# The recurrence's gate products written as three fp32r products of divided operands

## The chip, the cores and the metric

The kernel runs on one core of one Trainium2 chip. Its time is the device time of one execution in microseconds (us). A core has a matrix engine (PE, TensorE), a vector engine (DVE), an activation engine (ACT), a general engine (POOL, GpSimd) and a queue engine (SP) that here issues every DMA. The engines run side by side, each in its own program order, and wait for each other through semaphores.

## What is computed

One layer of a hybrid model on 1280 tokens: 1024 latent tokens and 256 context tokens, of width 1024. A projection feeds three branches: a long convolution (Hyena), a Fourier mixing (FNet) and a bidirectional gated recurrence (RG-LRU). Then follow a merge, an output projection and a feed-forward part. The change is in the recurrence. Cut to what matters:

```python
def rglru_scan(x, w_r, b_r, w_i, b_i, lam, h0, reverse, reset):
    xb = x.reshape(B, L, N_RG_BLOCKS, RG_BLOCK)          # 8 blocks of 128 channels
    r = sigmoid(einsum('blnc,ncd->blnd', xb, w_r) + b_r)
    i = sigmoid(einsum('blnc,ncd->blnd', xb, w_i) + b_i)
    log_a = -RG_C * r * softplus(-lam)
    a = exp(log_a)
    mult = sqrt(-expm1(2.0 * log_a))
    h = scan(h[t] = a[t] * h[t-1] + mult[t] * (i[t] * x[t]))   # forward and backward

xr = depthwise_conv(u_rx, rcw, rcb, ...)                  # 4 taps along the tokens
h_f = rglru_scan(xr, wr[0], ..., False, reset)
h_b = rglru_scan(xr, wr[1], ..., True, reset)
y_c = ((h_f + h_b) * gelu(u_ry)) @ w_c
```

The einsums are the gate products: in each of the 8 blocks, xr (128 channels by 1280 tokens) meets four 128x128 matrices, one for r and one for i in each direction.

## The kernel before

The activations lie with channels on the 128 partitions and tokens along the row. The 1280 tokens are cut in three pieces of 512, 512 and 256 columns. All big projections run as "split products": a weight tile and the input are each divided into a rounded part (fp32r, "hi") and the remainder ("lo"), and three fp32r matmuls, hi*hi, hi*lo and lo*hi, are added up in PSUM (`split_product`, lines 860 to 862). The input pairs h_hi and h_lo are made once. The weight tiles come from memory one by one: SP loads tile t into one of two buffers w_raw, POOL makes w_hi and w_lo from it in two instructions (lines 789 and 792), PE uses them. A tile of 128x1024 makes eight split products on each piece.

The stage of the change is the second one, `Fori(0, KD // 2) as m` with two halves s on every engine: eight passes n = 2m + s, one for each channel block of the recurrence, each with two projection tiles. What each engine does in pass n, in its order:

- PE: tile 2n+16 (it gives the recurrence's input `rin`), in an odd pass the FNet token matmuls, tile 2n+17 (it gives `g_ry`), a wait for xr, the 12 gate products (line 1042, plain fp32 in one call each), and in an even pass the FNet channel matmuls (line 1013).
- ACT: `rin` from PSUM (line 1247), FNet token copies in an odd pass, a wait for the pass before to have ended (`zc_ready`), gelu into `g_ry` (1316), 12 sigmoids that take the gate products (1324), then exp, tanh, square and root (1330 to 1336), and FNet copies in an even pass.
- DVE: the depthwise convolution that makes xr (1588, 1593), in an even pass the FNet first stage (lines 244 to 256, its result `fn_a` is PE's input at line 1013), then the recurrence (1712 to 1731). At its end it raises `zc_ready`. Only then does it start on the xr of the next pass.
- SP: it waits for `zc_ready` of the pass, stores the result, and only then issues the loads of the following pass: in its order FNet's input, the next `rpack` and the two weight tiles. `rpack` holds the four gate matrices and the vectors of a block; that of pass n is loaded during pass n-1.
- POOL: one loop that rounds and divides tile after tile. For tile t it waits until PE has finished tile t-2 (`proj_done[2]`), whose buffers it reuses, and until the new raw tile has landed.

So in pass n POOL divides tiles 2n+18 and 2n+19, the two of the next pass, whose loads SP issues after pass n-1 has ended.

In the trace a pass begins when DVE has ended the one before: the ends of passes 0, 1, 2 and 3 stand at 633.1, 680.7, 723.7 and 772.8 us. From pass 2 on, an even and an odd pass together take the same time again, 92.1 us.

Of the kernel before, what the change touches and what calls it, by code (L numbers as in the profile page):

```python
# [8 lines left out]
F32 = mybir.dt.float32  # L28
# [31 lines left out]

# [7 lines left out]

# [11 lines left out]

# [8 lines left out]


def real_dft_even(o, z, temp, out):


    e, d = temp(0, 4), temp(4, 8)
    o.add(e, z(0, 4), z(4, 8))
    o.sub(d, z(0, 4), z(4, 8))
    o.sub(out("re4"), temp(0), temp(2))
    o.sub(out("im4"), temp(3), temp(1))
    o.add(temp(8, 10), temp(0, 2), temp(2, 4))
    o.sub(temp(10), temp(5), temp(7))  # L100
    o.add(temp(11), temp(5), temp(7))
    o.add(out("re0"), temp(8), temp(9))
    o.sub(out("re8"), temp(8), temp(9))
    o.mul_add(out("re2"), temp(10), COS[2], temp(4))
    o.mul_add(out("re6"), temp(10), -COS[2], temp(4))
    o.mul_add(out("im6"), temp(11), -COS[2], temp(6))
    o.mul_sub(out("im2"), temp(11), -COS[2], temp(6))

# [28 lines left out]

# [6 lines left out]

# [46 lines left out]

# [7 lines left out]

class Chain:  # L200


# [9 lines left out]
    def loose(self, ins):  # L212


        ins.then_inc(self.sem, 1)
        self.n += 1
        if self.n > 1:
            self.eng.wait_ge(self.sem, self.n - 1)
# [16 lines left out]

class Butterfly:


# [19 lines left out]

class MixUnits:


# [17 lines left out]

# [10 lines left out]

def spectrum_places(buf):


    def at(name):
        if name.startswith("c"):
            return buf[:, 9 + int(name[3:]), :] if name[1:3] == "re" else buf[:, 19, :]
        f = int(name[2:])
        return buf[:, f if name[:2] == "re" else 11 + f, :]
    return at

# [14 lines left out]


# [4 lines left out]


def build_program(nc, dr):

    ctx = ExitStack()
    with ctx:
        def sem(name):
            return ctx.enter_context(nc.semaphore(name))

        def sb(stack, name, shape, dt=F32):  # L330
            return stack.enter_context(nc.sbuf_tensor(name, shape, dt))

# [20 lines left out]

# [49 lines left out]
        rpack = [sb(st, f"rpack{s}", [P, R_ALL]) for s in range(2)]  # L403
        for buf, name in ((r_b, "r_b"), (i_b, "i_b"), (a_b, "a_b")):
            buf.append(sb(st, f"{name}1", [P, T]))
# [14 lines left out]

# [15 lines left out]

# [9 lines left out]


# [21 lines left out]

# [45 lines left out]
        xr_ready = sem("xr_ready")  # L515
# [23 lines left out]


# [19 lines left out]
        def raw_z(n):  # L560


            if n == 2:
                return v_b, v_in, 16 * (CH + 1), 0
            if n < 2:
                return zraw[n], zraw_in[n], 16, 0
            slot = (n - 3) % 2
            return zraw[slot], zraw_in[slot], 16 * ((n - 3) // 2 + 2), n - 2 if n < 5 else n - 1
# [3 lines left out]

# [75 lines left out]

# [31 lines left out]

# [6 lines left out]

# [45 lines left out]

# [39 lines left out]


        @block.gpsimd
        def _(pool):
# [51 lines left out]
            with pool.Fori(TILES_L1 // 2 + 1, OUT_TILE0 // 2 + 1) as m:  # L828
                for s in range(2):

                    pool.wait_ge(proj_done[2], 2 * m + s)
                    split(2 * m + s, s, w_hi[s], w_lo[s])
# [6 lines left out]
            for q in range(FFN_TILES):  # L839


                if q < 2:
                    pool.wait_ge(proj_done[2], OUT_TILE0 + 1 + 31 + q)
                split(MIX_TILES + q, q, wf_hi[q], wf_lo[q])
# [7 lines left out]


        @block.tensor
        def _(pe):
# [8 lines left out]
            def projection(use, ws, xs, cols, made=None, pieces=(0, 1, 2)):  # L864


                for b in pieces:
                    a, e, _ = PIECES[b]

                    pe.wait_ge(proj_free[b], use)  # L870
                    for k, (w, x) in enumerate(zip(ws, xs)):
                        if made:
                            pe.wait_ge(made, len(xs) * b + k + 1)
                        ins = split_product(ps[b][:, 0:e - a], [w[0][:, cols[k]], w[1][:, cols[k]]],
                                            [x[0][:, a:e], x[1][:, a:e]], k == 0, k == len(ws) - 1)
                    ins.then_inc(proj_done[b], 1)
# [34 lines left out]

# [29 lines left out]

# [53 lines left out]

# [34 lines left out]
            with pe.Fori(0, KD // 2) as m:  # L1030
                for s in range(2):
                    n = 2 * m + s
                    projection_tile(2 * n + L2_TILE0, 0)
                    if s == 1:
                        fnet_tokens(m)
                    projection_tile(2 * n + (L2_TILE0 + 1), 1)
                    pe.wait_ge(xr_ready, n + 2)
                    pe.wait_ge(rpack_in[s], 16 * m + 16)
                    for j in range(12):
                        out, done = mix_unit(u2, m, RG_UNIT[s] + j)  # L1040
                        a, e, _ = PIECES[j % 3]
                        mm(out[:, 0:e - a], rpack[s][:, (j // 3) * P:(j // 3 + 1) * P], xr[:, a:e],
                           start=True, stop=True).then_inc(done, 1)
                    if s == 0:
                        fnet_channels(m)

# [42 lines left out]

# [36 lines left out]

# [41 lines left out]

        @block.scalar
        def _(act):  # L1170
# [15 lines left out]

# [53 lines left out]

# [39 lines left out]

# [24 lines left out]
            with act.Fori(0, KD // 2) as m:  # L1305
                for s in range(2):
# [4 lines left out]
                    if s == 1:  # L1311
                        take_fnet_tokens(m)
                    act.wait_ge(zc_ready, n + 1)
# [26 lines left out]

# [38 lines left out]

# [30 lines left out]

# [34 lines left out]

# [16 lines left out]


        @block.vector
        def _(dve):
# [16 lines left out]

# [28 lines left out]


# [170 lines left out]

# [15 lines left out]
            with dve.Fori(0, KD // 2) as m:  # L1699
                for s in range(2):  # L1700
# [5 lines left out]
                              pack[:, R_CONVB:R_CONVB + 1], 4, 2, xr_ready)  # L1706
                    if s == 0:
                        fnet_first_stage(m)
# [25 lines left out]

# [36 lines left out]

# [79 lines left out]

# [65 lines left out]


def dft_constants():

# [23 lines left out]

# [14 lines left out]

# [3 lines left out]

# [5 lines left out]

# [75 lines left out]
```

## Time and profile before

| | before |
|---|---|
| device time, median of 3 runs (lowest, highest) | 2820.89 us (2819.37, 2822.51) |
| span of the profiled execution, first to last instruction | 2818.3 us |
| PE busy | 2576.4 us, 91% |
| PE loading weights | 2141.8 us, 76% |
| DVE busy | 1579.7 us, 56% |
| POOL busy | 884.1 us, 31% |
| ACT busy | 559.6 us, 20% |
| mean granted PE clock | 0.961 |

The span is 2.6 us shorter than the median of the timed runs: what lies around the span. Busy shares are averages over stages with different limits. The stage of the change runs from about 572 to 957 us. PE's matmuls are pipelined, so that two in a row overlap in the records; the distance between two starts is what one costs. An fp32 matmul leaves two records for each call. A clock of 1.00 is 2.4 GHz and one of 0.50 is 1.2 GHz.

### The profile page before, as it was taken

The page shows a single profiled execution, that of the slowest core. Times are in us where ns is not written, and L with a number is a line of the kernel's source. Part 1 is how long each engine was busy: PE and PEld are TensorE (multiplying, and loading weights), DVE is VectorE, ACT ScalarE, POOL GpSimd, SP SyncE. Part 2 cuts the span into 40 slices and gives each one's busy share as a digit, 9 for nine tenths or more (in the row PEclk, how much of TensorE's full clock was granted, in tenths as well). Part 3 has the DMA queues.
Part 4 walks back from the last instruction along what each step waited for, and adds up shares of the span by engine and source line. Part 5 has one row for each costly group of instructions (what it writes and reads, how often), then busy time and mean ns, then how long its engine had stood idle before and what let it go on. Part 6 is the DMA issues. An engine that isn't in the chain of part 4 may idle for free. (4 is left out here: it accounts for less than half of the span.)

```text
span 2818.3 us, 34644 instructions
## 1 busy us (share of the span) xinstructions
PE 2576.4 (91%) x13422; PEld 2141.8 (76%) x13422; DVE 1579.7 (56%) x2636; ACT 559.6 (20%) x825; POOL 884.1 (31%) x483
## 2 busy tenths in 40 slices
PE   6599998999999799999987998979999999999995
PEld 2377776786877688878876887858888888888885
DVE  6888888856568466665666445383322233332227
ACT  3201101045565421122221001130000000000002
POOL 0355455622121122322232332333323133323220
PEclk9799999999999899999998999989999999999998
DMA  6222333122112322222235323211011011101002
GB/s 263 79 96 105 127 122 126 56 96 75 44 68 70 144 92 99 100 91 91 91 119 207 129 86 103 84 45 45 30 45 35 24 45 45 45 30 45 22 22 75
DMA packets 53536, 233.49 MB, mean 83 GB/s; under 512 B 6628, under 2 KB 8548, under 8 KB 47861
## 3 DMA queue, kind: packets, MB, share of 16 engines
q1 hardware_dynamic: 53492, 232.93, 23.0%
q8 instruction: 26, 0.43, 0.1%
q14 instruction: 18, 0.14, 0.0%
HBM read 178.37 MB, written 54.53 MB: 83 GB/s over the span
## 5 line engine op out<-in xcount | busy, mean ns | idle before, releaser
L860 PE MATMUL ps<-h_hi,w_hi 128*128 128x512 f32 (+1 forms) x2256 | 812.1, 360 | 42.5 <-DVE h_lo L1570 18.4
L861 PE MATMUL ps<-h_lo,w_hi 128*128 128x512 f32 (+1 forms) x2256 | 802.4, 356 | 0.0
L862 PE MATMUL ps<-h_hi,w_lo 128*128 128x512 f32 (+1 forms) x2256 | 801.6, 355 | 0.0
L789 POOL TENSOR_TENSOR w_hi<-w_raw,zero_col 128x1024 fp32r<-128x1024 f32 x102 | 229.2, 2247 | 1576.3 <-PE ps L862 1118.0
L860 PEld LDWEIGHTS ps<-h_hi,w_hi 128*128 128x128 f32 x2256 | 428.4, 190 | 116.8 <-issue 28.9
L862 PEld LDWEIGHTS ps<-h_hi,w_lo 128*128 128x128 f32 x2256 | 428.3, 190 | 60.6
L861 PEld LDWEIGHTS ps<-h_lo,w_hi 128*128 128x128 f32 x2256 | 428.9, 190 | 58.4
L1862 DVE TENSOR_TENSOR a<-sil,ps 128x512 f32<-128x512 f32 (+1 forms) x66 | 39.5, 598 | 506.2 <-PE ps L862 505.0
L792 POOL TENSOR_TENSOR w_lo<-w_raw,w_hi 128x1024 fp32r<-128x1024 f32 x102 | 277.1, 2716 | 8.0
L1896 DVE SCALAR_TENSOR_TENSOR x<-ps,mod,x 128x512 f32<-128x512 f32 (+1 forms) x264 | 172.1, 661 | 95.0 <-PE ps L862 94.4
L861 PE MATMUL ps<-h_lo,wf_hi 128*128 128x512 f32 (+1 forms) x528 | 188.7, 357 | 0.0
L860 PE MATMUL ps<-h_hi,wf_hi 128*128 128x512 f32 (+1 forms) x528 | 188.7, 357 | 0.0
L862 PE MATMUL ps<-h_hi,wf_lo 128*128 128x512 f32 (+1 forms) x528 | 188.7, 357 | 0.0
L862 PE MATMUL ps<-act_hi,wf_lo 128*128 128x512 f32 (+1 forms) x528 | 187.0, 354 | 0.0
L861 PE MATMUL ps<-act_lo,wf_hi 128*128 128x512 f32 (+1 forms) x528 | 187.0, 354 | 0.0
L860 PE MATMUL ps<-act_hi,wf_hi 128*128 128x512 f32 (+1 forms) x528 | 186.8, 354 | 0.0
L1429 ACT ACTIVATE sil<-ps 128x512 f32<-128x512 f32 (+1 forms) x66 | 34.7, 527 | 763.1 <-PE ps L862 763.1
L789 POOL TENSOR_TENSOR wf_hi<-w_raw,zero_col 128x1024 fp32r<-128x1024 f32 x44 | 86.2, 1960 | 180.0 <-PE ps L862 180.0
L953 PE MATMUL ps<-f_a,fwd 128*128 128x128 f32 x640 | 90.1, 310 | 53.9 <-DVEq L1650 53.3
L953 PEld LDWEIGHTS ps<-f_a,fwd 128*128 128x128 f32 x640 | 87.9, 225 | 57.3 <-issue 50.3
L860 PEld LDWEIGHTS ps<-h_hi,wf_hi 128*128 128x128 f32 x528 | 100.0, 189 | 15.7
L862 PEld LDWEIGHTS ps<-h_hi,wf_lo 128*128 128x128 f32 x528 | 99.3, 188 | 15.9
(238 smaller groups left out, 3807.7 us busy)
## 6 DMA issues: line engine op xcount, KB each, us to landing
w_raw<-in_weights SPq DMA_DIRECT2D x146, 512.0 KB, 3.7
ada_w<-in_w_ada SPq DMA_DIRECT2D x20, 1024.0 KB, 6.2
scratch_gate_s<-g_st SPq DMA_DIRECT2D x24, 640.0 KB, 3.3
side<-scratch_gate_s SPq DMA_DIRECT2D x24, 640.0 KB, 3.9
scratch_k_s<-kstage SPq DMA_DIRECT2D x8, 1536.0 KB, 5.1
hy_k<-scratch_k_s SPq DMA_DIRECT2D x8, 1536.0 KB, 8.8
scratch_hy_s<-hout SPq DMA_DIRECT2D x16, 640.0 KB, 3.2
x_in<-in_x SPq DMA_DIRECT2D x8, 640.0 KB, 9.1
```

Of the source, the lines that this page charges most:

```text
L789: nc.gpsimd.tensor_tensor(hi[:], w_raw[slot % 2][:], zero_col[:].to_broadcast([P, D]), ALU.add).then_inc(pool_step, 1)
L792: nc.gpsimd.tensor_tensor(lo[:], w_raw[slot % 2][:], hi[:].bitcast(F32), ALU.subtract).then_inc(split_done, 1)
L860: mm(out, w_pair[0], x_pair[0], start=first, stop=False)
L861: mm(out, w_pair[0], x_pair[1], start=False, stop=False)
L862: return mm(out, w_pair[1], x_pair[0], start=False, stop=last)
L953: ins = mm(o, mats[:, q, m, :], part, start=n == 0, stop=n == len(terms) - 1)
L1429: fn(sil[n % 2][:, 0:e - a], ps[b][:, 0:e - a], ACT.Silu).then_inc(f_free[b], 1)
L1862: tt(a32[n % 2][:, 0:e - a], sil[n % 2][:, 0:e - a], ps[ub][:, 0:e - a], ALU.mult).then_inc(f_free[ub], 1)
L1896: stt(x1[:, m, a:e], ps[b][:, 0:e - a], mod[:, 5 * KD + m, seq:seq + 1], x1[:, m, a:e], ALU.mult, ALU.add).then_inc(f_free[b], 1)
```

## The change

It does these things:

- the gate matrices of a pass are divided by POOL into `rm_hi` and `rm_lo` (128x512 each), in two new instructions between the division of tile 2n+18 and that of tile 2n+19; there is one pair of buffers for all passes
- xr is divided into `xr_hi` by ACT (one copy of 128x1280, after it has waited for xr, ahead of the gelu) and into `xr_lo` by DVE (one subtraction of 128x1280, after it has waited for `xr_hi`, ahead of FNet's first stage)
- PE waits for both divisions, and each of the 12 fp32 gate products becomes three fp32r matmuls
- the DMA scratch (`dynamic_dma_scratch_size`) is set to 2048, which makes room for the new buffers

```diff
+        xr_hi, xr_lo = sb(st, "xr_hi", [P, T], F32R), sb(st, "xr_lo", [P, T], F32R)
+        rm_hi, rm_lo = sb(st, "rm_hi", [P, 4 * P], F32R), sb(st, "rm_lo", [P, 4 * P], F32R)
...
         def _(pool):
-            with pool.Fori(TILES_L1 // 2 + 1, OUT_TILE0 // 2 + 1) as m:
+            def split_gates(n, s, loads):
+                pool.wait_ge(rpack_in[s], loads)
+                nc.gpsimd.tensor_tensor(rm_hi[:], rpack[s][:, 0:4 * P], zero_col[:].to_broadcast([P, 4 * P]),
+                                        ALU.add).then_inc(rm_rounded, 1)
+                pool.wait_ge(rm_rounded, n + 1)
+                nc.gpsimd.tensor_tensor(rm_lo[:], rpack[s][:, 0:4 * P], rm_hi[:].bitcast(F32),
+                                        ALU.subtract).then_inc(rm_split, 1)
+            with pool.Fori(0, KD // 2) as m:
+                for s in range(2):
+                    n = 2 * m + s
+                    for q in range(2):
+                        pool.wait_ge(proj_done[2], 2 * n + (TILES_L1 + 2 + q))
+                        split(2 * n + (TILES_L1 + 2 + q), q, w_hi[q], w_lo[q])
+                        if q == 0:
+                            split_gates(n, s, 16 * m + 16)
+            with pool.Fori((TILES_L1 + TILES_L2) // 2 + 1, OUT_TILE0 // 2 + 1) as m:
...
         def _(pe):
-                    pe.wait_ge(xr_ready, n + 2)
-                    pe.wait_ge(rpack_in[s], 16 * m + 16)
+                    pe.wait_ge(xr_split, n + 1)
+                    pe.wait_ge(rm_split, n + 1)
                     for j in range(12):
                         out, done = mix_unit(u2, m, RG_UNIT[s] + j)
                         a, e, _ = PIECES[j % 3]
-                        mm(out[:, 0:e - a], rpack[s][:, (j // 3) * P:(j // 3 + 1) * P], xr[:, a:e],
-                           start=True, stop=True).then_inc(done, 1)
+                        cols = slice((j // 3) * P, (j // 3 + 1) * P)
+                        split_product(out[:, 0:e - a], [rm_hi[:, cols], rm_lo[:, cols]],
+                                      [xr_hi[:, a:e], xr_lo[:, a:e]], True, True).then_inc(done, 1)
...
         def _(act):
+                    act.wait_ge(xr_ready, n + 2)
+                    fn(xr_hi[:], xr[:], ACT.Copy).then_inc(xr_rounded, 1)
                     act.wait_ge(zc_ready, n + 1)
...
         def _(dve):
+                    dve.wait_ge(xr_rounded, n + 1)
+                    tt(xr_lo[:], xr[:], xr_hi[:].bitcast(F32), ALU.subtract).then_inc(xr_split, 1)
...
-    nc = bacc.Bacc("TRN2", target_bir_lowering=False, num_devices=1)
+    nc = bacc.Bacc("TRN2", target_bir_lowering=False, num_devices=1, dynamic_dma_scratch_size=2048)
```

On POOL, in one odd pass of the second stage, the order of before is this (w_raw is the landed weight tile; raw_in0 and raw_in1 are the landings of its two buffers, proj_done2 is PE's end of a tile):

```order
L788 ISA [waits proj_done2]
L789 TENSOR_TENSOR w_hi<-w_raw,zero_col 128x1024 [waits raw_in0]
L791 REGISTER_ALU
L792 TENSOR_TENSOR w_lo<-w_raw,w_hi 128x1024 [waits pool_step]
L788 ISA [waits proj_done2]
L789 TENSOR_TENSOR w_hi<-w_raw,zero_col 128x1024 [waits raw_in1]
L791 REGISTER_ALU
L792 TENSOR_TENSOR w_lo<-w_raw,w_hi 128x1024 [waits pool_step]
```

The same place of the changed kernel:

```order
L729 ISA [waits proj_done2]
L730 TENSOR_TENSOR w_hi<-w_raw,zero_col 128x1024 [waits raw_in0]
L732 REGISTER_ALU
L733 TENSOR_TENSOR w_lo<-w_raw,w_hi 128x1024 [waits pool_step]
L773 TENSOR_TENSOR rm_hi<-rpack,zero_col 128x512 [waits rpack_in1]
L775 REGISTER_ALU
L776 TENSOR_TENSOR rm_lo<-rpack,rm_hi 128x512 [waits rm_rounded]
L729 ISA [waits proj_done2]
L730 TENSOR_TENSOR w_hi<-w_raw,zero_col 128x1024 [waits raw_in1]
L732 REGISTER_ALU
L733 TENSOR_TENSOR w_lo<-w_raw,w_hi 128x1024 [waits pool_step]
```

The division of this pass's gate matrices stands behind the division of the next pass's first tile, and with it behind that tile's landing.

On PE, at the end of a pass's second tile, the order of before:

```order
L862 MATMUL ps<-h_hi,w_lo 128x256
L1037 REGISTER_ALU
L1038 ISA [waits xr_ready]
L888 ISA [waits rpack_in0]
L1042 MATMUL ps<-xr,rpack 128x512 [waits mix_free0]
L1042 MATMUL ps<-xr,rpack 128x512 [waits mix_free1]
```

And of the changed kernel:

```order
L820 MATMUL ps<-h_hi,w_lo 128x256
L991 REGISTER_ALU
L845 ISA [waits rm_split,xr_split]
L818 MATMUL ps<-xr_hi,rm_hi 128x512 [waits mix_free0]
L819 MATMUL ps<-xr_lo,rm_hi 128x512
L820 MATMUL ps<-xr_hi,rm_lo 128x512
```

The wait for xr and for the landed rpack has become a wait for what DVE and POOL make of them.

On DVE, behind the convolution in an even pass, the order of before:

```order
L1593 SCALAR_TENSOR_TENSOR xr<-rin,rpack,xr 128x1024 [waits dve_step]
L1593 SCALAR_TENSOR_TENSOR xr<-rin,rpack,xr 128x256
L244 TENSOR_TENSOR fn_c<-fn_u 128x512 [waits dve_step,fn_in]
L247 TENSOR_TENSOR fn_c<-fn_u 128x512 [waits dve_step]
```

And of the changed kernel:

```order
L1535 SCALAR_TENSOR_TENSOR xr<-rin,rpack,xr 128x1024 [waits dve_step]
L1535 SCALAR_TENSOR_TENSOR xr<-rin,rpack,xr 128x256
L1648 REGISTER_ALU [waits dve_step]
L1649 TENSOR_TENSOR xr_lo<-xr,xr_hi 128x1280 [waits xr_rounded]
L208 TENSOR_TENSOR fn_c<-fn_u 128x512 [waits fn_in]
L211 TENSOR_TENSOR fn_c<-fn_u 128x512 [waits dve_step]
```

FNet's first stage now stands behind ACT's rounding of xr and behind the subtraction.

## Rows read from the trace of the kernel before

**Rows 1.** The page: its head, then its first part, the engines' busy times.
```profile
span 2818.3 us, 34644 instructions
...
PE 2576.4 (91%) x13422; PEld 2141.8 (76%) x13422; DVE 1579.7 (56%) x2636; ACT 559.6 (20%) x825; POOL 884.1 (31%) x483
```

**Rows 2.** Who waited for whom, on PE: us in total, times, longest.
```profile
PE ps L1064 <- DMA v_b<-scratch_hy_s: 16.8, 1, 16.8
...
PE ps L1042 <- DVEq L1596: 13.1, 3, 4.4
```

**Rows 3.** Timeline of DVE, passes 1 to 3: start, length, what, [idle before].
```profile
679.19 1.49 DVE L1731 TENSOR_TENSOR r_b<-r_b,g_ry 128x1280 f32<-128x1280 f32 x1 [0.22 <-DVE r_b L1729]
...
682.82 5.12 DVE L1593 SCALAR_TENSOR_TENSOR xr<-rin,rpack,xr 128x1024 f32<-128x1024 f32 x6
...
691.41 2.57 DVE L244 TENSOR_TENSOR fn_c<-fn_c 128x256 f32<-128x256 f32 x1
...
699.57 0.28 DVE L247 TENSOR_TENSOR fn_a<-fn_u 128x128 f32<-128x128 f32 x1
...
722.23 1.49 DVE L1731 TENSOR_TENSOR r_b<-r_b,g_ry 128x1280 f32<-128x1280 f32 x1 [0.22 <-DVE r_b L1729]
...
725.42 5.11 DVE L1593 SCALAR_TENSOR_TENSOR xr<-rin,rpack,xr 128x1024 f32<-128x1024 f32 x6
```

**Rows 4.** Timeline of PE around the gate products of pass 3, an odd one.
```profile
735.97 0.39 PE L862 MATMUL ps<-h_hi,w_lo 128*128 128x512 f32 x1
736.20 0.28 PE L860 MATMUL ps<-h_hi,w_hi 128*128 128x256 f32 x1
736.31 0.28 PE L861 MATMUL ps<-h_lo,w_hi 128*128 128x256 f32 x1
...
739.07 8.75 PE L1042 MATMUL ps<-xr,rpack 128*128 128x512 f32 x24
747.47 0.58 PE L860 MATMUL ps<-h_hi,w_hi 128*128 128x512 f32 x1
```

**Rows 5.** Timeline of all engines in pass 2, an even one: ACT and PE.
```profile
698.38 1.05 ACT L1324 ACTIVATE i_b<-ps,rpack 128x512 f32<-128x512 f32 x2 [0.17 <-PE ps L1042]
...
700.02 7.17 PE L1013 MATMUL ps<-fn_ch,fn_a 128*128 128x256 f32 x32 [1.25 <-DVEq L1697]
...
703.39 1.27 ACT L1333 ACTIVATE r_b<-a_b 128x1280 f32<-128x1280 f32 x1
```

**Rows 6.** Timeline of POOL: passes 0, 2 and 3.
```profile
597.90 2.53 POOL L789 TENSOR_TENSOR w_hi<-w_raw,zero_col 128x1024 fp32r<-128x1024 f32 x1 [26.57 <-DMA w_raw<-in_weights]
...
604.79 3.48 POOL L792 TENSOR_TENSOR w_lo<-w_raw,w_hi 128x1024 fp32r<-128x1024 f32 x1
...
689.06 2.07 POOL L789 TENSOR_TENSOR w_hi<-w_raw,zero_col 128x1024 fp32r<-128x1024 f32 x1 [37.44 <-DMA w_raw<-in_weights]
691.22 2.48 POOL L792 TENSOR_TENSOR w_lo<-w_raw,w_hi 128x1024 fp32r<-128x1024 f32 x1
...
730.44 1.89 POOL L789 TENSOR_TENSOR w_hi<-w_raw,zero_col 128x1024 fp32r<-128x1024 f32 x1 [32.15 <-DMA w_raw<-in_weights]
```

**Rows 7.** Timeline of SP, pass 2: the issue of the next pass's two weight tiles.
```profile
683.13 0.86 SPq L578 DMA_DIRECT2D w_raw<-in_weights  x2
```

**Rows 8.** Timeline of DVE, pass 0.
```profile
604.57 1.49 DVE L1712 TENSOR_TENSOR i_b<-i_b,xr 128x1280 f32<-128x1280 f32 x1 [5.90 <-ACT i_b L1324]
```

**Rows 9.** Groups by line, POOL, shapes apart: count, busy us, mean ns.
```profile
L813 POOL TENSOR_TENSOR hout<-hout,hy_part 128x256 f32<-128x256 f32 x80 | 68.4, 855 | 6.7
```

**Rows 10.** Timeline of PE, pass 0.
```profile
599.42 8.76 PE L1042 MATMUL ps<-xr,rpack 128*128 128x512 f32 x24
608.02 7.07 PE L1013 MATMUL ps<-fn_ch,fn_a 128*128 128x256 f32 x32
```

**Rows 11.** Sums by stretch: length, busy of PE, PEld, DVE, ACT, POOL, granted clock.
```profile
688.00:692.00 4.00, 3.78 (x7) 1.88 (x8) 3.91 (x5) 1.34 (x2) 2.86 (x2) 0.62 0.35 143
...
255.00:259.00 4.00, 4.00 (x19) 4.00 (x20) 3.63 (x3) 0.00 (x0) 3.63 (x5) 0.52 0.17 72
```

More of the change, by code:

```diff
@@ L513, in build_program @@
         k_ready = sem("k_ready")
-        xr_ready = sem("xr_ready")
+        xr_ready, xr_rounded, xr_split = sem("xr_ready"), sem("xr_rounded"), sem("xr_split")
+        rm_rounded, rm_split = sem("rm_rounded"), sem("rm_split")
         a2_ready = sem("a2_ready")
```

## The prediction

> **What bounds the kernel now.** I read the page first: PE is busy 91% of the span, DVE 56%, POOL 31% [rows 1]. That makes PE the engine to save on, and gate products that cost less would be a gain. But the share is an average, so I went to the waits of PE next, to see whether PE sets the end in the stage that is changed. It doesn't quite: three times PE stands 4.4 us in front of the gate products, 13.1 us in all, until DVE has made xr, and at the end of the stage it stands 16.8 us for a load that SP issues only after the last pass of DVE [rows 2]. So the end of the stage is the end of DVE's pass 7, and every wait of PE before it counts only by what it does to that.
>
> The timelines show the loop behind it. Pass 1 ends on DVE at 680.7, the convolution that makes xr runs until 687.9, pass 2 ends at 723.7, and the convolution of pass 3 runs until 730.5 [rows 3]. In an even pass PE waits for xr, its gate products end at 698.8, ACT's last sigmoid at 699.4, and the FNet channel matmuls start at 700.0, when DVE has ended FNet's first stage [rows 3, 5]. Two tiles later PE reaches the gate products of pass 3 at 739.1, 8.5 us after xr is there: odd passes are bound by PE. The end of an odd pass follows its sigmoids at a fixed distance and starts the next even one. That loop, all engines in turn, is the bound.
>
> **The matmuls themselves: a gain.** A block of 12 gate products takes 8.4 us at full clock, from 739.07 to 747.47 [rows 4]. In fp32r, matmuls start 0.23 us apart at 512 columns and 0.12 apart at 256 [rows 4]. A block then has 24 of the first and 12 of the second: 24 x 0.227 + 12 x 0.12 = 6.9 us. That is 1.5 us less, and in an odd pass the first fp32r matmul behind the block, 0.58 us long in place of 0.39, gives some 0.2 back too. ACT follows the products and could take off a little less; I take 1.6 us for an odd pass and 1.5 for an even one. Were nothing else changed, the eight blocks would give 12 to 13 us.
>
> **The division of xr: two steps ahead of PE and of FNet.** ACT's copy of 128x1280 costs 1.3 us, as the square of the same size [rows 5], DVE's subtraction 1.5 us, as the product of the same size [rows 8]; with two hand-overs xr is divided 3.0 us after it is made. In odd passes the 8.5 us of slack hide it. In even passes it would put the gate products at 690.9 instead of 688.2. ACT's gelu and sigmoid table load, which now stand behind the copy, are done by 693.5. Behind DVE's wait is FNet's first stage, and it starts 3 us later.
>
> **The division of the gate matrices: where the wait is.** POOL executes in order. It divides the next pass's first tile, then this pass's gate matrices. That tile's load is issued by SP after the end of the pass before, at 683.1 in pass 2 [rows 7], and POOL, idle for 37.4 us, starts on it at 689.06 [rows 6]. The gate matrices were loaded a pass ago, but they are queued behind it. Counting on POOL: w_hi 1.9 to 2.1, w_lo 2.35 to 2.5 [rows 6], then two instructions of 512 columns. No row has these; half of the large ones is 1.0 and 1.2 us, and an instruction of 256 columns takes 0.86 [rows 9], so together they lie between 1.7 and 4.5. I take 2.3, half of the large ones, since the small one lies only little below. Undisturbed, the gate matrices are ready 6.8 us after the landing: 695.8.
>
> It won't be undisturbed. While POOL works, DVE's small operations of some 0.4 us are stretched to 2.57 us [rows 3], about the length of one POOL instruction; and a POOL w_lo that started 0.2 us into DVE's 1.49 us product took 3.48 instead of 2.4 [rows 6, 8]. So the two alternate by whole instructions. xr_lo now falls into POOL's w_hi, runs when that has ended, and holds up w_lo by 1.5 us; one or two FNet operations get in between, 0.7 us. That gives 698.0 for the start of the gate products in pass 2, 9.8 us later than before.
>
> The Trainium skill, "SBUF — State Buffer", section "Who interferes with whom", says that a DVE instruction with two SBUF inputs and a GpSimd instruction that reads SBUF exclude each other for a whole instruction. By that rule xr_lo costs POOL its full 1.5 us and 698.0 stands; without it the undisturbed 695.8 would be the number. The trace agrees, with the 3.48 us.
>
> From there: the block takes 6.9 us plus what the clock takes. After the 4.4 us wait of before, the granted clock was 0.62 in the 4 us behind it, and after a 6.2 us wait of an earlier stage it was 0.52 in the 4 us behind it [rows 11]; either way some 3.4 to 4 us of work at 1.2 GHz, or 1.7 to 2 us lost. In pass 2 that loss was there before. So the block ends at 698.0 + 6.9 + 1.7 = 706.6, 7.8 us later than 698.8. DVE has ended FNet's first stage by about 705, since POOL is at work until 703. The FNet matmuls start at 706.8 instead of 700.0: PE goes on 6.8 us later, and the pass, behind its sigmoids, ends 7.8 us later.
>
> **The odd pass behind it.** PE arrives at 745.9 instead of 739.1. POOL, from a landing at 730.4 + 7.8, needs 6.7 us and up to 1.5 more for xr_lo: 744.9 to 746.4. That is a draw; I add 0.3. The block saves 1.6. So an even and an odd pass together take 6.8 + 0.3 - 1.6 = 5.5 us more. There are three such pairs (passes 2 to 7): 16.5 us.
>
> **The first pair.** In pass 0 nothing waited. The tile lands at 597.90 [rows 6], the gate products started at 599.42 [rows 10]. Now they start 7.4 us after the landing, at 605.3, 5.9 us later, with a wait long enough to lose the clock: 6.9 + 2.0 us for the block, which ends at 614.2 instead of 608.0 [rows 10], 6.2 us later. In pass 1 the draw again, 0.7 here, minus 1.6: 5.3 us.
>
> **The rest.** The DMA scratch: every transfer of this kernel is issued by SP, none by POOL, and no row prices the scratch; I take nothing. The same page, section "SBUF size: 192, 224, or 256?", says that this scratch belongs to descriptors made on GpSimd, which no run here shows. The tiles 2n+19, divided after the gate matrices, are ready at 703 and needed at about 732. The later stages start from the load at the end of pass 7 [rows 2] and are only shifted.
>
> **Sum.** 5.3 + 16.5 = 21.8 us. The span of 2818.3 us [rows 1] becomes 2840.1; with the 2.6 us around it, which the median has too, 2842.7, so 2843.
>
> Bounds: with an undisturbed POOL (695.8) and no draw lost, a pair costs 4.5 - 1.6 = 2.9 and the first 3.8: 12.5 us, 2833. With more DVE operations in between (699.5) and 1.5 us lost in each odd pass, a pair costs 8.2 and the first 7.5: 32 us, 2853.
>
> **The rivals.** First, POOL is not late, and only the division of xr stands in the way. Then an even block starts at 690.9 and ends 0.8 us later than before; FNet's stage, 3 us later under POOL's work, puts PE 2.6 us back, less 1.6 in the odd pass: 1.0 us a pair, and the first pair gains 3.2. Together about 0: 2821. For it: odd passes have slack and the matrices lie there early. Against it: the order of POOL and the landing at 689.06 after an idle time of 37 us. 7 in 100.
>
> Second, faster: both divisions are hidden and the blocks give their 12 to 13 us, 2808. It needs the gate matrices and xr divided before PE arrives at 683.8 in an even pass, when xr is only made at 687.9. 6 in 100.
>
> Third, slower still: the clock. With 14 us of waiting in an even pass PE might run the whole block at 1.2 GHz, 6.9 us lost in place of 1.7, in four passes: 20 us more, 2863. It decides from the point where the clock stays low for over 4 us of work after a wait; the 6.2 us wait of an earlier stage shows 4 [rows 11]. 7 in 100.
>
> **How the numbers follow.** The forecast with its bounds has 80 in 100, the rivals 20. The range of 2833 to 2853 is the forecast's own; I widen it by 2 us below for a landing that comes sooner: 2831 to 2853. Beyond about 0.2%, 5.6 us, a measurement of this kernel can tell a change. Slower takes in the forecast and the third rival, 0.87; within 0.2%: 0.07; faster: 0.06.
>
> **What would show it.** In the profile after, the longest waits of PE before the gate products should end on POOL's rm_lo, four of them in even passes, some 14 us each in passes 2, 4 and 6 and 6 us in pass 0; small ones in odd passes. POOL's order should show w_hi, w_lo, rm_hi, rm_lo directly behind the landing. A pair should take 97.6 us instead of 92.1. A block should take 6.9 us in odd passes. If PE waits for xr_lo instead, the first rival holds; if it doesn't wait at all, the second.

## The result

The changed kernel takes 2842.28 us, the median of 4 runs (2839.52 to 2848.59), beside 2821.33 us for the kernel before. The ratio is 1.0077, with a 95% interval of 1.0063 to 1.0091: it is slower by 21 us, or 0.8%. The forecast was 2843 us. The four runs lie 9 us apart, and the profiled one is the fastest of them (2839.5 us).

The page of the changed kernel, its head and the busy times, beside [rows 1]:

```profile
span 2837.7 us, 34885 instructions
...
PE 2566.2 (90%) x13518; PEld 2155.8 (76%) x13518; DVE 1611.1 (57%) x2644; ACT 569.3 (20%) x833; POOL 911.0 (32%) x499
```

PE is busy for 10 us less than before, in a span that is 19 us longer. The gain on the matmuls is there and doesn't decide the time. The waits of PE, beside [rows 2] (us in total, times, longest):

```profile
PE ps L818 <- POOL rm_lo L776: 46.1, 4, 14.6
...
PE ps L1018 <- DMA v_b<-scratch_hy_s: 16.7, 1, 16.7
```

The three waits for xr, 13.1 us, are gone. Four waits for POOL's rm_lo, 46.1 us, stand in their place. The wait for v_b at the end of the stage is as long as before, so the stage in front of it has grown as a whole: the first matmul on v_b starts at 984.6 us in place of 962.6, 22.0 us later.

POOL in passes 2 and 3, beside [rows 6] (start, length, what, idle before):

```profile
691.11 1.89 POOL L730 TENSOR_TENSOR w_hi<-w_raw,zero_col 128x1024 fp32r<-128x1024 f32 x1 [36.13 <-DMA w_raw<-in_weights]
693.08 3.47 POOL L733 TENSOR_TENSOR w_lo<-w_raw,w_hi 128x1024 fp32r<-128x1024 f32 x1
696.51 1.49 POOL L773 TENSOR_TENSOR rm_hi<-rpack,zero_col 128x512 fp32r<-128x512 f32 x1
698.08 1.59 POOL L776 TENSOR_TENSOR rm_lo<-rpack,rm_hi 128x512 fp32r<-128x512 f32 x1
699.63 1.94 POOL L730 TENSOR_TENSOR w_hi<-w_raw,zero_col 128x1024 fp32r<-128x1024 f32 x1
...
747.54 1.28 POOL L776 TENSOR_TENSOR rm_lo<-rpack,rm_hi 128x512 fp32r<-128x512 f32 x1
```

The gate matrices had been loaded in the pass before, and POOL stood idle for 36 us. It was waiting for the landing of a tile of the next pass, which nobody needed yet. And PE, where those instructions end:

```profile
699.90 0.79 PE L818 MATMUL ps<-xr_hi,rm_hi 128*128 128x512 f32 x1 [13.76 <-POOL rm_lo L776]
...
709.32 2.97 PE L967 MATMUL ps<-fn_ch,fn_a 128*128 128x256 f32 x13
```

The gate products start when rm_lo has ended. On DVE, xr_lo fell into POOL's w_hi and then held up w_lo:

```profile
691.65 2.71 DVE L1649 TENSOR_TENSOR xr_lo<-xr,xr_hi 128x1280 fp32r<-128x1280 f32 x1 [1.39 <-ACT xr_hi L1262]
```

It takes 2.71 us instead of 1.49, and w_lo 3.47 instead of about 2.4.

### The profile page after: what moved, and what is told of

It reads as the page before. It is cut to its first block and busy times, and to the rows that moved or that the text cites. A ratio compares the mean times of both kernels' runs of the same rounds, so it can differ in the third digit from the quotient of the medians.

```text
span 2837.7 us, 34885 instructions
## 1 busy us (share of the span) xinstructions
PE 2566.2 (90%) x13518; PEld 2155.8 (76%) x13518; DVE 1611.1 (57%) x2644; ACT 569.3 (20%) x833; POOL 911.0 (32%) x499
## 5 line engine op out<-in xcount | busy, mean ns | idle before, releaser
L1802 DVE TENSOR_TENSOR a<-sil,ps 128x512 f32<-128x512 f32 (+1 forms) x66 | 39.5, 599 | 506.2 <-PE ps L820 505.0
L820 PEld LDWEIGHTS ps<-h_hi,wf_lo 128*128 128x128 f32 x528 | 99.2, 188 | 15.9
```

What stands on the lines that cost most here:

```text
L820: return mm(out, w_pair[1], x_pair[0], start=False, stop=last)
L1802: tt(a32[n % 2][:, 0:e - a], sil[n % 2][:, 0:e - a], ps[ub][:, 0:e - a], ALU.mult).then_inc(f_free[ub], 1)
```

## The experiments

Each was timed in 4 to 11 runs beside the kernel before on the same chip. The diffs are against the changed kernel, those of before_early and before_scratch against the kernel before. "Pair" is an even and an odd pass, from the end of one odd pass to the end of the next on DVE (instruction r_b<-r_b,g_ry). It is 92.1 us in the kernel before and 98.2 to 99.6 in the changed one.

| run | time, us | ratio (95%) | pairs, us |
|---|---|---|---|
| changed kernel | 2842.3 | 1.0077 (1.0063 to 1.0091) | 98.2, 99.6, 98.4 |
| rm_alone | 2849.8 | 1.0098 (1.0083 to 1.0114) | 99.2, 99.1, 98.8 |
| early_loads | 2840.0 | 1.0064 (1.0050 to 1.0078) | 99.1, 99.1, 92.4 |
| before_early | 2834.8 | 1.0050 (1.0037 to 1.0064) | 97.5, 98.3, 93.1 |
| xr_alone | 2830.7 | 1.0027 (1.0018 to 1.0036) | 94.7, 95.2, 95.1 |
| gates_first | 2826.3 | 1.0022 (1.0012 to 1.0031) | 94.5, 95.0, 93.2 |
| before_scratch | 2821.0 | 1.0001 (0.9992 to 1.0010) | 92.1, 92.1, 92.1 |
| all_vector | 2819.8 | 0.9995 (0.9986 to 1.0004) | 93.2, 95.1, 92.9 |
| odd_vector | 2818.1 | 0.9989 (0.9980 to 0.9998) | 90.8, 90.8, 90.8 |
| odd_queue | 2816.3 | 0.9986 (0.9977 to 0.9995) | 90.8, 90.8, 90.8 |

**Gate matrices first (gates_first).** POOL's two instructions are swapped ahead of the tile; everything else is the changed kernel.

```diff
                     for q in range(2):
                         pool.wait_ge(proj_done[2], 2 * n + (TILES_L1 + 2 + q))
-                        split(2 * n + (TILES_L1 + 2 + q), q, w_hi[q], w_lo[q])
                         if q == 0:
                             split_gates(n, s, 16 * m + 16)
+                        split(2 * n + (TILES_L1 + 2 + q), q, w_hi[q], w_lo[q])
```

> The changed kernel with one thing moved: POOL divides the gate matrices of the pass before it divides the tile behind which they were queued. The same instructions run. Queue theory (the loss comes from the gate matrices' place behind the landing of a tile): in even passes PE now waits only for xr_lo, which ends about 11.4 us after the pass before, where rm_lo ended at 16.9; the FNet matmuls then start about 1.3 us later than in the kernel before and an odd block saves 1.6, so a pair takes 91.8 us instead of 98; passes 0 and 1 gain 3. Time about 2817 us, within 2812 to 2822. Work theory (the added work of ACT, DVE and POOL and their mutual exclusion costs it): all of that is still there, so most of the 20 us stays, 2833 or more.

It took 2826.3 us. 16 of the 21 us are gone with the same instructions, so the place in the queue carries most of the loss and the work theory falls. But it is above the 2812 to 2822 of the queue theory too. The trace shows where the rest is. PE starts the gate products of pass 2 11.3 us after the end of pass 1, as expected, but goes on to the FNet matmuls 2.0 us later than in the kernel before (2.6 and 2.5 in passes 4 and 6), where 1.3 was expected. The larger part lies elsewhere. POOL is no longer held back by the landing and divides the gate matrices as soon as PE has ended the tile. For the gate matrices of passes 2, 4 and 6 that moment lies in DVE's scans of the pass before (pass 3 here, POOL, then DVE):

```profile
763.56 1.25 POOL L773 TENSOR_TENSOR rm_hi<-rpack,zero_col 128x512 fp32r<-128x512 f32 x1 [16.34 <-PE ps L820]
764.88 3.16 POOL L776 TENSOR_TENSOR rm_lo<-rpack,rm_hi 128x512 fp32r<-128x512 f32 x1
```

```profile
763.94 3.01 DVE L1667 TENSOR_TENSOR_SCAN t_b<-a_b,rpack,i_b 128x1024 f32<-128x1024 f32 x1
766.88 1.72 DVE L1667 TENSOR_TENSOR_SCAN t_b<-a_b,i_b 128x256 f32<-128x256 f32 x1
```

The scans take 2.35 and 0.67 us where POOL is idle; here 3.01 and 1.72. The end of the odd pass, which the loop waits for, moves by 1.7 us in each of passes 1, 3 and 5.

**Tile loads earlier (early_loads).** POOL's order is that of the changed kernel; SP issues the loads earlier.

```diff
-                    load_ahead(2 * n + L2_TILE0, 0)
-                    load_ahead(2 * n + (L2_TILE0 + 1), 1)
...
+                    if not (last and s):
+                        load_ahead(2 * n + (L2_TILE0 + 2), 0)
+                        load_ahead(2 * n + (L2_TILE0 + 3), 1)
                     sp.wait_ge(zc_ready, n + 2)
...
+            load_ahead(L2_TILE0, 0)
+            load_ahead(L2_TILE0 + 1, 1)
             sp.wait_ge(hy_stored, 16 * TILES_L1)
```

> The changed kernel with POOL's order left as it is and SP's changed: SP issues the two tile loads of a pass before it waits for the end of the pass ahead, and those of pass 0 before FNet's input. Queue theory: the tile has landed when PE gives its buffer free, so rm_lo is ready long before PE asks, although its place in the queue is the same; POOL's work also moves away from xr_lo and FNet's first stage. PE waits for xr_lo, some 10.2 us after the end of the pass before; a pair takes about 90 us. Time 2812 to 2818 us. If the place in POOL's order itself costs, or the added work, it stays at 2833 or more.

It took 2840.0 us: a clear miss. Half of the theory is borne out: but for 1.2 us in pass 0 no matmul waits for rm_lo any longer, and in passes 2, 4 and 6 PE's waits for the gate products end on xr_lo, 11.2 us after the end of the pass before. In odd passes, too, the gate products start sooner (10.8 us after the end of the pass before, instead of 14.4). Still a pair takes 99 us, since the ends of the passes are late. POOL and DVE, at the end of pass 3:

```profile
769.02 2.26 POOL L733 TENSOR_TENSOR w_hi<-w_raw,zero_col 128x1024 fp32r<-128x1024 f32 x1 [16.90 <-PE ps L823]
771.36 4.26 POOL L736 TENSOR_TENSOR w_lo<-w_raw,w_hi 128x1024 fp32r<-128x1024 f32 x1
775.58 1.42 POOL L776 TENSOR_TENSOR rm_hi<-rpack,zero_col 128x512 fp32r<-128x512 f32 x1
```

```profile
769.56 3.87 DVE L1670 TENSOR_TENSOR_SCAN t_b<-a_b,rpack,i_b 128x1024 f32<-128x1024 f32 x1
773.35 2.81 DVE L1670 TENSOR_TENSOR_SCAN t_b<-a_b,i_b 128x256 f32<-128x256 f32 x1
776.11 0.06 DVE L1665 MEMSET r_b<- 128x1 f32 x1
776.22 2.13 DVE L1666 TENSOR_TENSOR i_b<-r_b,i_b 128x1280 f32<-128x1280 f32 x1
778.38 3.26 DVE L1670 TENSOR_TENSOR_SCAN t_b<-a_b,rpack,i_b 128x1024 f32<-128x1024 f32 x1
```

Four DVE operations of 2.35, 0.67, 1.49 and 2.35 us take 3.87, 2.81, 2.13 and 3.26: 5.2 us more on the path. The last instruction of the pass meets POOL's next tile and takes 2.88 us instead of 1.49, and that of an even pass takes 3.39. From the start of its gate products pass 3 needs 39.5 us, where it needs 32.3 in the changed kernel. The price of POOL's place in the queue was replaced by the price of POOL's work under the scans. The last pair, 92.4 us, agrees: in pass 7 no tile load is left to bring POOL's work forward, and its scans have their usual lengths.

**Only the gate matrices' division (rm_alone).** The products stay in fp32 and read the undivided operands; rm_hi and rm_lo are made, waited for and not used.

```diff
-                    pe.wait_ge(xr_split, n + 1)
+                    pe.wait_ge(xr_ready, n + 2)
+                    pe.wait_ge(rpack_in[s], 16 * m + 16)
                     pe.wait_ge(rm_split, n + 1)
                     for j in range(12):
...
-                        cols = slice((j // 3) * P, (j // 3 + 1) * P)
-                        split_product(out[:, 0:e - a], [rm_hi[:, cols], rm_lo[:, cols]],
-                                      [xr_hi[:, a:e], xr_lo[:, a:e]], True, True).then_inc(done, 1)
+                        mm(out[:, 0:e - a], rpack[s][:, (j // 3) * P:(j // 3 + 1) * P], xr[:, a:e],
+                           start=True, stop=True).then_inc(done, 1)
...
-                    act.wait_ge(xr_ready, n + 2)
-                    fn(xr_hi[:], xr[:], ACT.Copy).then_inc(xr_rounded, 1)
...
-                    dve.wait_ge(xr_rounded, n + 1)
-                    tt(xr_lo[:], xr[:], xr_hi[:].bitcast(F32), ALU.subtract).then_inc(xr_split, 1)
```

> The kernel before with POOL's division of the gate matrices in its changed place, and PE waiting for it; the products stay in fp32 and read the undivided operands, and xr is not divided, so rm_hi and rm_lo are made and not used. Queue theory: the gate products of passes 2, 4 and 6 start some 15.4 us after the end of the pass before instead of 7.5 and nothing is saved on them: 6.8 us for each pair and some 5 us in pass 0. Time about 2846 us, 2840 to 2852. Work theory: POOL's 16 small instructions take 27 us of an engine that is idle for two thirds, 2821 to 2825.

It took 2849.8 us, in the range of the queue theory, and is slower than the changed kernel. The waits of PE there:

```profile
PE ps L997 <- POOL rm_lo L776: 43.1, 4, 12.6
```

Sixteen small instructions on an engine that is idle most of the time cost 28 to 29 us (the first by the ratio, the second by the medians). The gate products of passes 2, 4 and 6 start 15.3 to 15.8 us after the end of the pass before, where 15.4 was expected.

**Only xr's division (xr_alone).** POOL as before, products in fp32; ACT and DVE divide xr and PE waits for xr_lo. xr_hi and xr_lo are not used.

```diff
-                        if q == 0:
-                            split_gates(n, s, 16 * m + 16)
...
                     pe.wait_ge(xr_split, n + 1)
-                    pe.wait_ge(rm_split, n + 1)
+                    pe.wait_ge(rpack_in[s], 16 * m + 16)
...
-                        cols = slice((j // 3) * P, (j // 3 + 1) * P)
-                        split_product(out[:, 0:e - a], [rm_hi[:, cols], rm_lo[:, cols]],
-                                      [xr_hi[:, a:e], xr_lo[:, a:e]], True, True).then_inc(done, 1)
+                        mm(out[:, 0:e - a], rpack[s][:, (j // 3) * P:(j // 3 + 1) * P], xr[:, a:e],
+                           start=True, stop=True).then_inc(done, 1)
```

> The kernel before with the division of xr by ACT and DVE, and PE waiting for xr_lo; the products stay in fp32 and read the undivided operands, and POOL is as before. The xr division by itself: in odd passes hidden by the 8.5 us of slack, in passes 2, 4 and 6 it delays the gate products by 3 to 4 us, since xr_lo meets POOL's w_hi. PE goes on 2.8 us later in each pair: 8 us, time about 2829, 2825 to 2832. If xr's division is what makes the changed kernel slow, this one stands at about 2840 or more.

2830.7 us, as expected: xr's division alone costs 8 to 10 us here (again by the ratio and by the medians), or 3 us for a pair. In the changed kernel PE doesn't wait for xr_lo itself, since rm_lo is later still; what is left of its price is what it does to POOL. The gate products of pass 2 start 16.9 us after the end of the pass before in the changed kernel and 15.8 in rm_alone; w_lo, which xr_lo holds up, takes 3.47 us and 2.47. So the two prices don't add up: 29 and 10 us by themselves, and 21 in the changed kernel, which has both and the gain on the products.

**The loads earlier, in the kernel before (before_early).** SP's edit of early_loads, made to the kernel before.

> The kernel before, nothing divided in addition, with SP issuing the two tile loads of a pass before it waits for the end of the pass ahead, as in the earlier run with early loads. A test of what made that run slow, free of gate matrices. Collision theory (POOL and DVE exclude each other for whole instructions, and POOL's work, no longer held back by a late landing, now falls into DVE's scans at the end of an odd pass, which the loop waits for): two POOL instructions there stretch the end of each odd pass by some 4 us, FNet's first stage is freed and gives back 1.2; a pair takes 94 to 96 us instead of 92.1; time 2827 to 2833 us. If landings only matter by being late, nothing is late in this kernel but FNet's stage: 2817.

2834.8 us, 2 us above the range, and on the side of the collision theory: the kernel before, too, gets slower when its tiles land sooner. A pair takes 97.5 us. POOL and DVE, at the end of pass 3:

```profile
766.18 1.89 POOL L792 TENSOR_TENSOR w_hi<-w_raw,zero_col 128x1024 fp32r<-128x1024 f32 x1 [18.06 <-PE ps L865]
768.15 4.26 POOL L795 TENSOR_TENSOR w_lo<-w_raw,w_hi 128x1024 fp32r<-128x1024 f32 x1
```

```profile
766.21 4.01 DVE L1727 TENSOR_TENSOR_SCAN t_b<-a_b,rpack,i_b 128x1024 f32<-128x1024 f32 x1
770.14 2.81 DVE L1727 TENSOR_TENSOR_SCAN t_b<-a_b,i_b 128x256 f32<-128x256 f32 x1
```

The two scans lose 3.8 us. What the estimate left out is POOL's second tile, which now meets the start of the convolution of the even pass: there xr is ready 9.8 us after the end of the pass before (790.8 after 781.0) instead of 7.2. The last instruction of an even pass is stretched too, from 1.49 to 3.38 us.

**The DMA scratch (before_scratch).**

```diff
-    nc = bacc.Bacc("TRN2", target_bir_lowering=False, num_devices=1)
+    nc = bacc.Bacc("TRN2", target_bir_lowering=False, num_devices=1, dynamic_dma_scratch_size=2048)
```

> The kernel before with the DMA scratch set to 2048 and nothing else. All theories: no change, 2821 us within 0.1%. If the scratch has a price, it is a part of the 21 us that nothing else in the trace would show.

2821.0 us, ratio 1.0001 (0.9992 to 1.0010), and every pair 92.1 us. No price of the scratch can be seen here. The trace also shows how far two traces of nearly the same kernel differ: pass 0 ends at 634.8 us instead of 633.1, and the span is 4.3 us longer.

**Who divides the gate matrices (all_vector).** The changed kernel, with POOL exactly as in the kernel before. ACT rounds the gate matrices, and DVE makes their remainder while it waits for ACT's rounding of xr.

```diff
         def _(pool):
-                        if q == 0:
-                            split_gates(n, s, 16 * m + 16)
...
         def _(act):
+                    act.wait_ge(rpack_in[s], 16 * m + 16)
+                    fn(rm_hi[:], rpack[s][:, 0:4 * P], ACT.Copy).then_inc(rm_rounded, 1)
                     act.wait_ge(xr_ready, n + 2)
...
         def _(dve):
+                    dve.wait_ge(rm_rounded, n + 1)
+                    tt(rm_lo[:], pack[:, 0:4 * P], rm_hi[:].bitcast(F32), ALU.subtract).then_inc(rm_split, 1)
                     dve.wait_ge(xr_rounded, n + 1)
```

> The changed kernel, split products in all eight passes, but with the gate matrices rounded by ACT and their remainder made by DVE while it waits for ACT's rounding of xr; POOL is exactly as in the kernel before. It differs from the run with the gate matrices first in nothing but who divides them. Collision theory: that run's 5 us over the kernel before come from POOL's two small instructions in DVE's scans at the end of a pass; without them the scans keep their lengths, PE waits in even passes for xr_lo alone, some 11.4 us after the pass before, a pair takes 92.5 to 93.2 us, and passes 0 and 1 gain 3 in all: 2820 us, 2817 to 2823. If xr's division alone explains that run, this one is at 2826 too.

2819.8 us: the 5 us that gates_first lay above the kernel before are gone, and with them the whole loss of the change. The scans at the end of pass 3 have their lengths again:

```profile
761.60 2.35 DVE L1669 TENSOR_TENSOR_SCAN t_b<-a_b,rpack,i_b 128x1024 f32<-128x1024 f32 x1
763.87 0.67 DVE L1669 TENSOR_TENSOR_SCAN t_b<-a_b,i_b 128x256 f32<-128x256 f32 x1
```

Pairs take 93.2, 95.1 and 92.9 us. The middle one is outside what was expected. In pass 4 PE waits 2.1 us for FNet's first stage, and the clock, which had come back in the gate products, is granted at 1.2 GHz once more, from 795.0 to 798.4 us:

```profile
794.60 8.86 PE L965 MATMUL ps<-fn_ch,fn_a 128*128 128x256 f32 x32 [2.11 <-DVEq L1638]
```

The FNet matmuls take 7.17 us in pass 6 of the same trace, so 1.7 of the 1.9 us between the first two pairs are here. With all eight blocks split and nothing queued behind a landing, the change is no gain: in pass 2 the FNet matmuls start 2.5 us later than in the kernel before, and the odd block gives back 1.3.

**Split products in odd passes alone (odd_queue, odd_vector).** Even passes keep the fp32 products and divide nothing. In odd_queue POOL divides the gate matrices in the changed kernel's place; in odd_vector ACT and DVE do. The divisions of xr, and in odd_queue POOL's `split_gates`, stand under `if s == 1`. The common core on PE:

```diff
-                    pe.wait_ge(xr_split, n + 1)
-                    pe.wait_ge(rm_split, n + 1)
+                    if s == 1:
+                        pe.wait_ge(xr_split, m + 1)
+                        pe.wait_ge(rm_split, m + 1)
+                    else:
+                        pe.wait_ge(xr_ready, n + 2)
+                        pe.wait_ge(rpack_in[s], 16 * m + 16)
...
+                        if s == 1:
+                            split_product(out[:, 0:e - a], [rm_hi[:, cols], rm_lo[:, cols]],
+                                          [xr_hi[:, a:e], xr_lo[:, a:e]], True, True).then_inc(done, 1)
+                        else:
+                            mm(out[:, 0:e - a], rpack[s][:, cols], xr[:, a:e],
+                               start=True, stop=True).then_inc(done, 1)
```

In odd_vector, besides:

```diff
+                        act.wait_ge(rpack_in[1], 16 * m + 16)
+                        fn(rm_hi[:], rpack[1][:, 0:4 * P], ACT.Copy).then_inc(rm_rounded, 1)
...
+                        dve.wait_ge(rm_rounded, m + 1)
+                        tt(rm_lo[:], rpack[1][:, 0:4 * P], rm_hi[:].bitcast(F32),
+                           ALU.subtract).then_inc(rm_split, 1)
```

> The split gate products only in odd passes, with the gate matrices divided by POOL in the same place as in the changed kernel; even passes are those of the kernel before. Queue and collision theories: in odd passes xr has 8.5 us of slack and the gate matrices are ready about when PE arrives, so each odd pass keeps its 1.6 us and nothing is paid in even ones, except up to 1.5 us of waiting in pass 1: a pair takes 90.5 to 91 us, time 2815 us, 2813 to 2819. If fp32r blocks gain nothing here, for instance because ACT's sigmoids set the pace, 2821.

> As the run with split products in odd passes alone, but with the gate matrices rounded by ACT and their remainder made by DVE, in the slack of an odd pass; POOL is exactly as in the kernel before. Nothing is queued behind a landing and POOL has no more work than before: 1.6 us in each of the four odd passes, 2814 to 2816 us. If POOL's share in the run beside it costs nothing, both are equal.

odd_queue took 2816.3 us, ratio 0.9986 (0.9977 to 0.9995), and odd_vector 2818.1, ratio 0.9989 (0.9980 to 0.9998), 2 us above its range. In the trace of each a pair takes 90.8 us, 1.3 less than 92.1, where 1.6 was expected. POOL in pass 3 of odd_queue:

```profile
734.83 2.29 POOL L773 TENSOR_TENSOR rm_hi<-rpack,zero_col 128x512 fp32r<-128x512 f32 x1
737.21 1.29 POOL L776 TENSOR_TENSOR rm_lo<-rpack,rm_hi 128x512 fp32r<-128x512 f32 x1
```

rm_lo ends at 738.5, PE starts the gate products at 739.5: in time, by 1 us. In pass 1 PE waits 1.2 us for it; up to 1.5 was expected. Both are a little faster than the kernel before. The intervals of the two overlap, so which of them is better isn't settled. The gain of odd_queue, 4 us, is smaller than 0.2%.

## Why the prediction was right, point by point

**Right: what bounds the stage.** The loop through DVE's end of pass, xr, the gate products, two tiles and the sigmoids. In rm_alone the FNet matmuls of pass 2, with which PE goes on, start 26.5 us after the end of pass 1 instead of 19.3, and a pair takes 7.1 us more; in xr_alone they start 22.1 us after it, and a pair takes 2.6 to 3.1 more.

**Right: the place of the loss.** Four waits on rm_lo in the even passes: 13.8, 14.6 and 13.9 us in passes 2, 4 and 6, where 14 was forecast, and 3.8 us in pass 0, where 6 was. That moving POOL's two instructions takes most of the loss away shows the cause.

**Right to a few tenths: the start.** In pass 2 the gate products were forecast 17.3 us after the end of pass 1 (698.0 after 680.7) and came 16.9 after it (699.90 after 682.99); in passes 4 and 6 it was 17.8 and 17.1. POOL's instructions of 512 columns, for which no row stood, took 1.04 and 1.26 us in pass 5, undisturbed; 1.0 and 1.2 were taken.

**DVE and POOL by turns.** An undisturbed POOL would have given 695.8, or 15.1 us after the end of pass 1; taking turns 698.0, or 17.3. The trace decides for the turns: xr_lo and w_lo were stretched by 1.2 and 1.1 us. By the rule of the Trainium skill, "SBUF — State Buffer", section "Who interferes with whom", a DVE instruction with two SBUF inputs and a GpSimd instruction that reads SBUF exclude each other for the whole instruction. The trace agrees with it, and so do the stretched scans of the experiments, 2.35 to 4.01 us.

**Mis-sized: the clock.** I took 1.7 us for the loss of clock in an even block. The granted clock of the changed kernel, in pass 2 (length, busy times, granted clock):

```profile
699.90:705.10 5.20, 5.20 (x14) 4.23 (x15) 5.20 (x7) 2.12 (x4) 4.30 (x2) 0.50 0.00 0
705.10:709.50 4.40, 4.40 (x25) 3.78 (x24) 2.65 (x7) 4.18 (x8) 0.00 (x0) 1.00 0.00 0
```

After 13.8 us of waiting PE works at 1.2 GHz for 5.2 us and loses 2.6. The block takes 9.4 us instead of 8.6. This is between the forecast and the third rival, which wanted the whole block at 1.2 GHz. A wait alone doesn't give the loss: after the same 4.4 us of waiting the block ran at 1.2 GHz for 3.4 us in the kernel before, and for 5.7 us in pass 4 of odd_queue, whose pair still takes 90.8 us. In pass 0 the forecast took 2.0 us for the clock; PE worked at 1.2 GHz for 3.4 us there and lost 1.7.

**Nearly right: the odd pass.** From the start of the gate products to the end of the pass 33.7 us became 32.3 (748.9 to 781.2): 1.4 saved, 1.6 forecast. The block itself, to the start of the next tile, takes 7.0 us (748.92 to 755.96), where 6.9 was forecast. The draw between PE and POOL went as said, with about half a microsecond lost in passes 1, 3 and 7 and 1.1 in pass 5:

```profile
748.15 0.28 PE L820 MATMUL ps<-h_hi,w_lo 128*128 128x256 f32 x1
748.92 0.47 PE L818 MATMUL ps<-xr_hi,rm_hi 128*128 128x512 f32 x1 [0.49 <-issue]
```

Together a pair was forecast at 97.6 us and took 98.2, 99.6 and 98.4. In the first, PE goes on with the FNet matmuls 7.0 us later after the end of the pass before (forecast 6.8), the draw costs 0.5 (0.3) and the odd block gives 1.4 (1.6): 6.1 in place of 5.5.

**Over-sized, by a landing: the first pair.** Forecast 5.3 us. Pass 1 ended at 682.99 instead of 680.68, 2.3 us later, in a trace whose first stage ended 0.9 us sooner, so some 3.2. The tile of pass 0 landed at 594.58 and not at 597.90. SP issues that load behind a store, which took 8.6 us there and 11.1 in the trace before; a single landing time was taken for a fixed one. In the other traces with the same order on SP that store took 8.2 to 11.7 us. With the landing of before, pass 1 would have ended about 5.6 us later (2.3 and the 3.3 us by which the tile came sooner, an estimate), so the steps of the forecast hold and the landing was luck.

**The sum.** Pass 7 ends at 979.1 instead of 956.9, 22.2 us later, for 21.8 forecast: 2.3 came by pass 1 and 19.9 in the three pairs, where 5.3 and 16.5 were forecast. The two errors cancel. The span grew by 19.4 us only, since what follows pass 7 is 2.8 us shorter, 1858.6 us instead of 1861.4. That is scatter as far as the traces tell: this stretch lies between 1856.8 and 1864.0 us in the eleven traces, and it is 1864.0 in before_scratch and 1861.4 in the kernel before. So the median, 0.7 us from the forecast, is closer than its terms, and closer than four runs that lie 9 us apart can bear out: that closeness is luck.

**The rivals.** The first, POOL in time and only xr's division in the way, didn't occur in the changed kernel, but two runs bring it about. With the gate matrices divided by POOL ahead of the tile (gates_first) it is 2826 in place of the 2821 that I gave it. It left out that POOL's two instructions then meet the scans, 1.7 us in each of three odd passes, and it gave the first pair a gain of 3.2 us, where pass 1 ended 1.4 us later. With the gate matrices divided by ACT and DVE (all_vector) the 2821 holds: 2820. The second, both divisions hidden, didn't occur; odd_queue and odd_vector show the part of it that is there to be had.

## What to carry to other kernels

An instruction put into an in-order queue costs what stands ahead of it, so look at what the instruction ahead waits for before its own length. Work on an engine that takes turns with the one that sets the pace has a right time as well: making it ready sooner can be worse than leaving it late, and both should be read off the timeline of the pacing engine. A cheaper operation is worth its preparation only where the preparation lies in slack; here that was every second pass, and the gain there, 4 us, is small.

## What the runs showed that I had not expected

The late landing of the tiles protected the kernel before. With nothing changed but the moment at which SP issues two loads, it got 0.5% slower (1.0037 to 1.0064), since POOL's 1.9 and 2.4 us instructions then met DVE's scans. Scans, products and the start of the convolution were all stretched: 2.35 to 4.01 us, 1.49 to 3.38, 1.14 to 3.71. Where both engines had work queued they took turns, one instruction each: a 0.67 us scan then took 2.81 us.
